# A decoder-step kernel: reordered queues in the first retrieval, and an output mixing whose matrix is loaded during the branches and whose input stays in SBUF

## The reference, cut to what matters

```
A  = dilated windowed attention over q, k, v of x W_in
Cv = B * conv3(C * x_in)
merged = sigmoid(gate_a) * (A @ w_branch_attn) + sigmoid(gate_c) * (Cv @ w_branch_conv)
h = LN1(alpha * x + merged @ w_out)
PEER: 8 heads; two 128-key score tables per head, top 16 of each, top 16 of the
      pair sums (eid, softmax g);  f = sum over (head, k) of g * gelu(h . u[eid]) * v[eid]
y = LN2(alpha * h + f)
```

## Time and profile before

| | |
|---|---|
| median of 3 runs | 4224.22 us (4220.33 to 4226.38) |
| profiled execution | 4224.69 us, span 4222.9 us |
| PE busy / DVE busy | 3685.5 us (87%) / 3001.5 us (71%) |
| ACT busy / POOL busy | 1240.1 us (29%) / 1843.2 us (44%) |
| DMA, mean | 243 GB/s |

### The profile page before, as it was taken

How to read it: one execution, slowest core, us unless ns; L and a number is a source line. 1 busy time by engine, 2 the same in 40 slices (tenths; PEclk the granted TensorE clock), 3 DMA queues, 4 the chain that set the end, 5 groups by cost and what they waited for, 6 DMA issues and landing times. The chain is left out here.

```text
span 4222.9 us, 64289 instructions
## 1 busy us (share of the span) xinstructions
PE 3685.5 (87%) x24855; PEld 3441.4 (81%) x24855; DVE 3001.5 (71%) x5899; ACT 1240.1 (29%) x2036; POOL 1843.2 (44%) x1382
## 2 busy tenths in 40 slices
PE   8999998997676399776773999999999999999998
PEld 8899896885555299764762889999999999999996
DVE  4434433333355668668687979999998999999996
ACT  2323313221233322211334952222222222222221
POOL 0000000000334435436576956666666666666661
PEclk9999998998777699988876999999999999999999
DMA  4122121896444278786201889999999999999996
GB/s 144 26 74 68 28 74 31 329 360 200 159 145 162 73 257 311 289 308 208 75 21 34 231 289 368 371 377 375 379 381 357 376 378 378 369 364 377 378 361 220
DMA packets 485059, 1024.51 MB, mean 243 GB/s; under 512 B 50977, under 2 KB 257441, under 8 KB 482841
## 3 DMA queue, kind: packets, MB, share of 16 engines
q0 software_dynamic: 149264, 543.49, 34.5%
q1 hardware_dynamic: 334264, 472.56, 32.5%
q10 hardware_dynamic: 1232, 4.46, 0.3%
HBM read 942.84 MB, written 131.28 MB: 254 GB/s over the span
## 5 line engine op out<-in xcount | busy, mean ns | idle before, releaser
L605 POOL DMA_INDIRECT u_row<-in_peer_u_dram,eid x512 | 731.6, 1429 | 646.0 <-DVE dots L623 556.5
L611 POOL DMA_INDIRECT v_row<-in_peer_v_dram,eid x512 | 583.5, 1140 | 193.4 <-issue 155.8
L640 DVE SCALAR_TENSOR_TENSOR f_row<-v_row,g_coef,f_row 128x1024 f32<-128x1024 f32 x508 | 661.4, 1302 | 1.5 <-DMA v_row<-in_peer_v_dram,eid 1.2
L81 PE MATMUL e_ps<-coef_h,v_h 128*128 128x288 f32 x2048 | 614.4, 300 | 44.9 <-DVE v_l L2318 28.2
L623 DVE CUSTOM_DVE_ANT_0 u_row<-u_row,h_row 128x1024 f32<-128x1024 f32 x512 | 630.9, 1233 | 5.0 <-DMA h_row<-s_h 2.7
L81 PE MATMUL e_ps<-tokens_Bh,u_h 128*128 128x288 f32 x2048 | 608.1, 297 | 7.0 <-DVE u_l L2312 7.0
L83 PE MATMUL e_ps<-coef_h,v_l 128*128 128x288 f32 x2048 | 609.8, 298 | 0.0
L82 PE MATMUL e_ps<-coef_l,v_h 128*128 128x288 f32 x2048 | 609.2, 297 | 0.0
L82 PE MATMUL e_ps<-tokens_Bl,u_h 128*128 128x288 f32 x2048 | 607.4, 297 | 0.0
L83 PE MATMUL e_ps<-tokens_Bh,u_l 128*128 128x288 f32 x2048 | 604.6, 295 | 0.0
L81 PEld LDWEIGHTS e_ps<-coef_h,v_h 128*128 128x128 f32 x2048 | 390.2, 191 | 57.1 <-DVE v_l L2318 36.3
(11 more groups left out here) (425 smaller groups left out, 8538.7 us busy)
## 6 DMA issues: line engine op xcount, KB each, us to landing
u_raw<-in_peer_uT_dram SPq DMA_DIRECT2D x128, 512.0 KB, 7.5
v_raw<-in_peer_vQ_dram SPq DMA_DIRECT2D x256, 256.0 KB, 6.6
s_g<-gate_block SPq DMA_DIRECT2D x9, 4096.0 KB, 16.3
x_gate<-s_g SPq DMA_DIRECT2D x64, 576.0 KB, 7.3
out_o_kv_sample_dram<-in_cache_kv_w_dram SPq DMA_DIRECT2D x32, 1016.0 KB, 8.0
c_rawA<-in_conv_tiles_dram SPq DMA_DIRECT2D x40, 512.0 KB, 5.6
c_rawB<-in_conv_tiles_dram SPq DMA_DIRECT2D x40, 512.0 KB, 6.3
w_raw<-in_w_in_dram SPq DMA_DIRECT2D x96, 192.0 KB, 3.7
```

The lines of the kernel that those rows point to most:

```text
L81: pe.matmul(out, lh, rh, start=first, stop=False)
L605: pool.indirect_dma_start(k["u_row"][:, r % RING], None, io["peer_u"][0], bass.IndirectOffsetOnAxis(ap=k["eid"][:, r:r + 1], axis=0)).then ...
L611: pool.indirect_dma_start(k["v_row"][:, v % RING], None, io["peer_v"][0], bass.IndirectOffsetOnAxis(ap=k["eid"][:, v:v + 1], axis=0)).then ...
L640: dve.scalar_tensor_tensor(out=f, in0=row, scalar=coef, in1=f, op0=ALU.mult, op1=ALU.add).then_inc(k["weighed"], 1)
```

## The change

1. `ROWS_IN` becomes (60, 16, 0): no row step in `mix_ln1` of B, so 16 more in `experts`.
2. The first branch weights (`load_branch(..., 0)`) are issued in the middle of `conv_gates`, at its unit 20 of 40; `r_raw` moves out of the phase to allow it.
3. `branches` writes the merged blocks to SBUF (`merged_at`) in place of storing them, and SP loads one row block of w_out after each block j, into a buffer for all eight.
4. `mix_ln1` reads both from SBUF. The split of a tile is now two instructions of half the size on ACT and on DVE. SP issues gain, bias and residuals only.
5. In `retrieve_early`, SP issues `load_new(i+1)` and `load_keys(i+1)` ahead of `load_values(i)`. ACT does the exponent and one-hot of head i-2 at the start and in the middle of iteration i, in place of its end. POOL does the distances first and each half of the look-up behind each half of the queries.

```diff
-ROWS_IN = (60, 16, 16)
+ROWS_IN = (60, 16, 0)
...
                 load(n + 5)
+                if n == NQ // 2:
+                    load_branch(sp, k, io, 0)
...
-            load_w(0)
             for s in range(SP):
...
             for j in range(KD):
                 load_w(j + 2)
                 load_gate(j + 2)
-                sp.wait_ge(br_done, NC * (j + 1))
-                sp.dma_start(io["s_merged"][j][:, cols], mg[:, j % 2]).then_inc(mg_out[j % 2], 16)
-            for x in range(2):
-                sp.wait_ge(mg_out[x], 16 * KD // 2)
+                sp.dma_start(k["w_out"][half.name][:, j], io["w_out"][0, j * P:(j + 1) * P]).then_inc(k["o_in"][j], 16)
...
-    at_row = spread(y0, rows, [1] * (TL - 1) + [0])
+    at_row = spread(y0, rows, [1] * TL)
...
-            load_tile(0)
-            for kk in range(KD):
-                if kk >= WB:
-                    sp.wait_ge(w_lo, kk - WB + 1)
-                sp.dma_start(wraw[:, kk % WB], io["w_out"][0, kk * P:(kk + 1) * P]).then_inc(wraw_in[kk % WB], 16)
...
+            N.load(sp)
+            for i in range(TL):
                 load_residual(i)
...
@@ retrieve_early, SP
-                load_values(i)
                 if i + 1 < DB:
                     load_new(i + 1)
                     load_keys(i + 1)
+                load_values(i)
@@ ACT
             for i in range(HEADS + 1):
+                if i >= 2:
+                    weights(i - 2)
+                    one_hot(i - 2, 0)
                 if i < HEADS:
                     query(i, 0)
                     split_w(i + 1, 0)
                 if i >= 1:
                     copy_probs(i - 1)
+                if i >= 2:
+                    one_hot(i - 2, 1)
...
-                if i >= 2:
-                    choose(i - 2)
@@ POOL
             for i in range(HEADS + 1):
-                if i < HEADS:
-                    for x in range(2):
+                if i >= 2:
+                    distances(i - 2)
+                for x in range(2):
+                    if i < HEADS:
                         query(i, x)
                         split_w(i + 1, x)
-                if i >= 2:
-                    look_up(i - 2)
+                    if i >= 2:
+                        look_up(i - 2, x)
```

More of the change, by code:

```diff
@@ L684, with load_branch, merged_at @@
 PIECES = [[(2, 4, 0)], [(2, 4, 1)], [(2, 4, 2)], [(2, 4, 3), (0, 1, 0)], [(1, 1, 0)]]
+def load_branch(sp, k, io, j):
+    wa, wc = (io[n][0].rearrange("(k p) (j c) -> j p k c", p=P, c=P) for n in ("w_branch_attn", "w_branch_conv"))
+    sp.dma_start(k["r_raw"][:, :SP], wa[j]).then_inc(k["r_raw_in"], 16)
+    sp.dma_start(k["r_raw"][:, SP:], wc[j]).then_inc(k["r_raw_in"], 16)
+def merged_at(k, half, j):
+    part, at = divmod(j, KD // 2)
+    return k["m" + half.name + "hl"[part]][:, KD // 2 + at]
 def conv_gates(nc, io, k, half, y0, rows):
@@ L1045, with __init__ @@
 class Norm:
[L1050 removed]
+    def __init__(self, nc, c, name, gain, bias, affine):
         def sb(n, s):
@@ L1173, in split @@
                 x, n = i % 2, n_of(i)
-                act.wait_ge(tile_in[x], 16 * (i // 2 + 1))
                 if i >= 2:
                     act.wait_ge(y_ready, i - 1)
-                act.activation(mh[:, x, :, :n], raw[:, x, :, :n], ACT.Copy).then_inc(m_hi, 1)
+                for part in range(2):
+                    m = act.activation(mh[:, x, part * KD // 2:(part + 1) * KD // 2, :n], merged(i, part), ACT.Copy)
+                m.then_inc(m_hi, 1)
             split(0)
             for kk in range(KD):
-                act.wait_ge(wraw_in[kk % WB], 16 * (kk // WB + 1))
-                act.activation(wh[:, kk], wraw[:, kk % WB], ACT.Copy).then_inc(w_hi, 1)
+                act.wait_ge(wraw_in[kk], 16 * (1 if half is EARLY else 2))
+                act.activation(wh[:, kk], wraw[:, kk], ACT.Copy).then_inc(w_hi, 1)
             act.wait_ge(N.eps_ready, 1)
@@ L1430, in scores, with weights, one_hot @@
                                    ACT.Copy).then_inc(s_copied, 1)
-            def choose(h):
+            def weights(h):
                 act.wait_ge(e_ready, h + 1)
                 act.activation(ex[:, h % 2], ex[:, h % 2], ACT.Exp).then_inc(e_done, 1)
-                for x in range(2):
-                    act.wait_ge(dist_ready, 2 * h + x + 1)
-                    act.activation(hot[:, x], hot[:, x], ACT.Square)
-                    act.drain()
-                    act.activation(hot[:, x], hot[:, x], ACT.Relu, bias=one[:], scale=-1.0).then_inc(hot_ready, 1)
+            def one_hot(h, x):
+                act.wait_ge(dist_ready, 2 * h + x + 1)
+                act.activation(hot[:, x], hot[:, x], ACT.Square)
+                act.drain()
+                act.activation(hot[:, x], hot[:, x], ACT.Relu, bias=one[:], scale=-1.0).then_inc(hot_ready, 1)
             def copy_queries(b):
@@ L1506, in _ @@
                     keep(i - 1)
-                if i >= 2:
-                    choose(i - 2)
-            choose(HEADS - 1)
+            weights(HEADS - 1)
+            for x in range(2):
+                one_hot(HEADS - 1, x)
         @block.gpsimd
@@ L2541, in program @@
              "cache_moved": c.enter_context(nc.semaphore("cache_moved"))}
+        with ExitStack() as alias:
+            for part in "hl":
+                k["mB" + part] = alias.enter_context(nc.sbuf_tensor("merged_B" + part, [P, KD, TB], F32))
         for part in "hl":
@@ L2557, in program @@
             k[n] = [nc.alloc_semaphore(f"{n}{x}") for x in range(count)]
+        k["w_out"] = {}
+        with ExitStack() as early:
+            early.enter_context(nc.sbuf_tensor("before_w_out_A", [P, words + 2 * KD * TA], F32))
+            k["w_out"]["A"] = early.enter_context(nc.sbuf_tensor("w_out_A", [P, KD, D], F32))
+        with ExitStack() as early:
+            early.enter_context(nc.sbuf_tensor("before_w_out_B", [P, words + 2 * KD * TB + (SP + KD) * P], F32))
+            k["w_out"]["B"] = early.enter_context(nc.sbuf_tensor("w_out_B", [P, KD, D], F32))
+        k["o_in"] = [nc.alloc_semaphore(f"o_in{x}") for x in range(KD)]
         done = 0
@@ L2573, in program @@
         first_sems = nc.snapshot_sems()
+        with ExitStack() as alias:
+            for part in "hl":
+                k["mA" + part] = alias.enter_context(nc.sbuf_tensor("merged_A" + part, [P, KD, TA], F32))
         with ExitStack() as first:
```

104 lines of the change are left out of this document (50 added, 54 removed).

## The result

The changed kernel takes 4069.13 us (median of 4 runs, 4068.73 to 4069.89) against 4222.62 us for the kernel before on the same chip (4220.33 to 4226.38). The ratio is 0.9636, interval 0.9619 to 0.9653. The prediction was 4085 us, range 4050 to 4138. The profiled execution took 4069.89 us, its span is 4068.1.

The account below looks back on a forecast made before the run. PE was taken to bound the phases, through its work or its waits for transfers, weights and DVE. Terms -79 - 8.5 - 2 - 16 - 50 + 16 = -139.5 against 4224.7 us gave 4085 us, range 4050 to 4138.

Parts of the forecast that it names:

- likeliest case: Whole kernel: the prediction's own forecast of 4085 us, with its own range 4070 to 4100, chance 0.50.
- clock rival: Both mixings and first retrieval: PE's clock stays at 2.4 GHz, period falls to 23.5 us, total 4065 us; chance 0.12.
- First retrieval, -79: First retrieval: PE's wait for `new` goes, period 37.76 to 26.0 us, last look-up wait goes; -79 us (-50 to -98).
- one hit of 2.1: First retrieval: one DVE instruction a period held up 2.1 us by a POOL one, lifting DVE's period to 26.2 us.
- ports: First retrieval: POOL's look-ups beside `pairs` take DVE's period to 30.4 us, saving only 53; total 4111 us; chance 0.18.
- Branches A, -8.5: Start of branches A: with weights already loaded, PE starts at 963.5 in place of 971.94; -8.5 us.
- Branches B, -2: Branches B: PE starts 4.9 us earlier, less 3 us for a fuller load queue; -2 us (-5 to +4).
- Mixing A, -16: Mixing A: first sum at 1065 in place of 1081.0, pitch and end kept; -16 us (-13 to -18.5).
- Mixing B, -50: Mixing B: first sum 23.7 us earlier, four pitches falling from 19.89 to 13.45 us (-25.8); -50 us (-45 to -54).
- Experts, +16: Experts: sixteen more row steps, one a group, each putting 1.1 us on the path; +16 us (+5 to +46).
- slower: Experts: every group stalls 9.8 us as DVE's slack shrinks and PE's clock falls, costing 157; total 4227 us; chance 0.03.
- two signs of being wrong: Prediction is wrong if `pairs` takes 4 us longer or more, or experts' groups grow by over 2.4 us.

Follow-up runs that it names:

- (72, 16, 0): The changed kernel with `ROWS_IN` = (72, 16, 0): twelve row steps of the experts done in conv B, which cost conv B 14.3 us.

## Why the prediction was right, step by step

It was right in sign and size: 4069 for 4085, 1 us below the likeliest case's own range (4070 to 4100), and inside the wide one. (The lower end of the wide range, 4050, is not what its working gives: the clock rival with the lower ends of the two mixings is 4065 - 6.5 = 4058.) By its own steps:

- **First retrieval, -79: measured -83.3.** The period of 26.0 was 25.8, the wait for `new` went, and DVE's idle time before the look-up's reduce went from 55.1 us in all to 9.8. That PE and DVE would tie at 26 was the step that failed: PE fell to 21.9 us as its clock rose from 0.76 to 0.95, and DVE alone sets the period. The number held because DVE's term, 24.05 and one hit of 2.1, stood at the same place. DVE's 24.05 plus the measured 1.25 of collisions make 25.3. The rivals "ports" and "clock" were thus each half true, and neither moved the period by what it named, 30.4 and 23.5. The argument against the first, that POOL has nothing to do at the short instructions of `pairs`, holds for the new order in the main: some 7 of the 29.5 us of excess lie in the instructions behind `candA` and its cast, against some 35 of 53.8 with the old order on POOL. That order, which the prediction meant to remove DVE's look-up wait, isn't needed for that (the wait is gone with SP's order alone); it keeps POOL out of DVE's way.
- **Branches A, -8.5: measured -7.7** at PE's first matmul (971.99 before), and 8.7 by undoing it.
- **Branches B, -2: measured about -5.** The seam gave its 4.9 (4.7 by undoing it). The 3 us that I took for a fuller queue didn't come: from the first matmul to mixing B's start there are 93.0 us before (1781.50 to 1874.52) and 92.3 after.
- **Mixing A, -16: measured -18.0** together with the branches' end. The first sum came 18.2 us after the start in place of 22, since the first tile's matmuls took 14.5 us and not 18.
- **Mixing B, -50: measured -54.3** with the seam ahead of it (-9.7 and -45.3, less the 0.7 of the branches themselves). First sum -27.3 for -23.7, by the same 14.5; pitches 13.2 for 13.45. The kernel before, without its row steps, shows the pitches' part alone: 26.7.
- **Second retrieval, 0: measured -5.8.** Not foreseen, and not explained; see below.
- **Experts, +16: measured +20.0.** That the size was nearly right is luck, since the working was not. It charged 1.1 us for each step. The runs show 0.3 to 0.5 us a step up to 28 a group, and 2.8 on average from 28 to 29. The share of DVE in the rows I had, 99.0 of 104.0 with 27 steps, held that knee: 99.0 + 2 x 2.5 = 104.0 is more than PE's 103.0. The rival "slower" argued from this margin, but made it a stall of 9.8 us in each group; a group beyond the knee costs 2.4.

The two signs of being wrong that the prediction named were met in single places: in the longest period the start of `pairs` takes 5 us longer than at its shortest, and the groups with 29 steps grow by about 3 us. On average they were not: 1.25 us a period, and 20 / 16 = 1.25 us a group.

The sum is -154.8 in place of -139.5. Of the 15 us more, 4 come from the first retrieval, 2 and 4 from the mixings, 3 from the branches, 6 from the second retrieval and 1 from the gates; the experts take 4 back.

## What to carry to other kernels

When a wait is taken out of a loop, ask of each engine how much work it has in the period that is left: the next bound may be one that is nowhere on the chain now, and PE's share shrinks by itself as its clock rises. The order of an engine off the path matters for what it runs beside. Filler work on a second engine was nearly free here until its work in a stage passed the first engine's, and cost its full length from then on; so count it per stage, compare the two sums, and stop one step short.

## What the runs showed that I had not expected

**The second retrieval has three lengths with the same code.** It took 262.8 to 265.5 us in nine kernels, 268.3 to 271.4 in four and 277.7 in one. It starts like the others, and single iterations differ. The third one in the new kernel, and the same in the kernel with (72, 16, 0):

```profile
1959.83:1987.26 27.43, 21.10 (x144) 20.73 (x144) 24.94 (x138) 11.32 (x19) 21.70 (x12) 0.85 0.13 39
```

```profile
1975.85:2007.01 31.16, 24.23 (x156) 23.86 (x155) 26.06 (x138) 11.45 (x19) 21.66 (x12) 0.84 0.15 44
```

DVE's work is the same within 1.1 us, and it stands idle for 2.6 us more; PE is busy for 3.1 us longer. The kernel before and its copy without row steps both have the long iteration (31.5 and 31.2), so it is not the row steps as such. What the phase inherits that decides this was not found. A change elsewhere can thus move this phase by 6 us, 0.15%, and one profile of each kernel can't separate that from an effect of its own.

**The first retrieval varies too.** Nine kernels with the same code for it took 245.3 to 253.8 us, with long periods (27.6 to 31) in other places, as POOL and DVE meet or miss each other. The changed kernel's 253.0 is the second longest of the nine, so its -83.3 stands near the small end of -82.5 to -91.0.
